# Latent attention of the first token tile split by key tile, with a running maximum, in a two-layer encoder kernel

## The reference

```
h = layer_norm(alpha * h + mixer(h))        # NA in layer 0, MLA in layer 1
hid = gelu(einsum('td,ted->te', h, u[experts]))
h = layer_norm(alpha * h + einsum('te,ted->td', gate * hid, v[experts]))

# MLA, all 16 heads, queries in blocks of 128
q = rms_norm(h @ w_q) @ w_q_up ; k, v = rms_norm(h @ w_kv) @ w_kv_up   (rope on 32 components of q and k)
p = softmax(q k^T * 96**-0.5) ; mix = (p v) @ w_out
```

## Time and profile before

| | us |
|---|---|
| median of 3 runs | 1616.34 (1616.20 to 1616.72) |
| profiled execution, its own time | 1621.26 |
| span of the profiled execution | 1619.5 |
| TensorE busy | 1373.9 (85%) |
| VectorE busy | 1056.7 (65%) |
| ScalarE busy | 476.5 (29%) |
| GpSimd busy | 490.3 (30%) |
| share of the chain that ended last: TensorE / DMA / VectorE | 36% / 34% / 22% |
| bytes read from HBM | 598.96 MB, 371 GB/s over the span |

### The profile page before, as it was taken

The page is one execution under the profiler, slowest core; times in us unless marked ns, Lnnn a source line. Parts: engine busy times, 40 slices in busy tenths (PEclk is TensorE's granted clock), DMA queues, the critical chain, the costliest instruction groups (busy, mean ns, idle before and its releaser), DMA issues.

```text
span 1619.5 us, 16307 instructions
## 1 busy us (share of the span) xinstructions
PE 1373.9 (85%) x5114; PEld 739.9 (46%) x5114; DVE 1056.7 (65%) x2834; ACT 476.5 (29%) x1237; POOL 490.3 (30%) x522
## 2 busy tenths in 40 slices
PE   8999888887878998897789868998877988887876
PEld 7887544433444454443254644444334433433322
DVE  1127777778867766777532477777776876776664
ACT  1122342334323332222123323333332222222222
POOL 0003233333433333333300123333333333333331
PEclk9999999999999999999998989999899999999999
DMA  9528999999999999999961299999999999999996
GB/s 344 189 97 329 387 419 421 418 421 405 398 423 414 420 421 418 417 408 415 419 246 40 94 399 421 407 402 420 420 396 420 420 405 421 421 422 422 412 418 258
DMA packets 92695, 601.09 MB, mean 371 GB/s; under 512 B 10433, under 2 KB 12737, under 8 KB 26433
## 3 DMA queue, kind: packets, MB, share of 16 engines
q0 software_dynamic: 73728, 536.90, 80.7%
q1 hardware_dynamic: 18880, 63.15, 10.1%
HBM read 598.96 MB, written 1.05 MB: 371 GB/s over the span
## 4 chain that ended last, share of the span: by engine, by line
PE 36%; DMA 34%; DVE 22%; issue 4%; ACT 2%; DVEq 2%; POOL 0%; another core or an unknown queue 0%; SPq 0%; POOLq 0%
DMA uv<-in_peer_uv_dram,expert 34%; PE y L554 17%; DVE uv L1417 11%; PE spare L452 3%; PE y L418 3%; PE px L327 2%; PE y L352 2%; ACT diag L1083 1%; DVE key_idx L1324 1%; DVE key_left L1316 1%; DVE key_idx L1318 1%; PE spare L383 1%; PE spare L382 1%; PE spare L369 1%; PE y L409 1%
## 5 line engine op out<-in xcount | busy, mean ns | idle before, releaser
L554 PE MATMUL y<-uv,diag 128*128 128x512 f32 x1928 | 923.4, 619 | 178.4 <-ACT diag L1083 175.1
L1417 DVE CUSTOM_DVE_ANT_0 uv<-px,uv 128x1024 f32<-128x1024 f32 x512 | 618.2, 1220 | 324.6 <-DMA uv<-in_peer_uv_dram,expert 320.3
L965 POOL DMA_INDIRECT uv<-in_peer_uv_dram,expert x512 | 489.1, 955 | 1105.6 <-PE y L554 844.7
L554 PEld LDWEIGHTS y<-uv,diag 128*128 128x128 f32 x1928 | 356.8, 196 | 639.4 <-issue 362.3
L1083 ACT ACTIVATE diag<-ident,wts 128x128 f32<-128x128 f32 x482 | 170.1, 396 | 449.1 <-DVE wts L1423 432.0
L1075 ACT ACTIVATE act_hid<-hid 128x2 f32<-128x2 f32 x260 | 53.4, 205 | 492.1 <-DVE hid L1417 491.8
L1075 ACT ACT_TABLE_LOAD x50 | 64.2, 1283 | 0.9
L398 PE MATMUL spare<-ident,probs 128*128 128x128 f32 x96 | 16.8, 301 | 35.8 <-DVE probs L1263 32.8
L1423 DVE TENSOR_TENSOR wts<-act_hid,gate 128x2 f32<-128x2 f32 x260 | 40.7, 157 | 7.5 <-ACT act_hid L1075 7.5
L1417 DVE DVE_READ_ACCUMULATOR2_ANT hid<- 128x1 f32 x512 | 42.5, 83 | 0.0
L1049 ACT ACT_TABLE_LOAD x30 | 38.5, 1283 | 0.5
(11 more groups left out here) (227 smaller groups left out, 1273.3 us busy)
## 6 DMA issues: line engine op xcount, KB each, us to landing
uv<-in_peer_uv_dram,expert POOLq DMA_INDIRECT x512
wb_rows<-in_peer_w_q_dram SPq DMA_DIRECT2D x16, 512.0 KB
uv<-in_na_w_dram SPq DMA_DIRECT2D x11, 512.0 KB, 8.9
wb_rows<-in_na_w_out_dram SPq DMA_DIRECT2D x8, 512.0 KB
uv<-in_mla_w_out_dram SPq DMA_DIRECT2D x8, 512.0 KB, 10.8
wb_rows<-in_mla_w_out_dram SPq DMA_DIRECT2D x8, 512.0 KB
bias<-in_na_bias_dram SPq DMA_DIRECT2D x16, 160.0 KB, 7.4
w_vu<-in_na_w_dram SPq DMA_DIRECT2D x4, 512.0 KB, 8.5
```

The costliest lines, as they stand in the source:

```text
L554: last = T.matmul(Y[t][:, c, :], diag[:, n % RING, :], uv[:, n % RING, 1, c * 512:(c + 1) * 512], start=False, stop=(k == TOPK - 1 and g % ...
L965: pool.indirect_dma_start(uv[:, n % RING, :, :].rearrange("p h d -> p (h d)"), None, uv_table, bass.IndirectOffsetOnAxis(ap=expert[:, g, k ...
L1417: V_.tensor_tensor_reduce(out=rows, in0=px[:, :, :], in1=rows, scale=1.0, scalar=0.0, op0=ALU.mult, op1=ALU.add, accum_out=hid[:, k:k + 1] ...
```

## The change

MLA of tile 0 is computed in two parts. The scores against tile 0's own 128 keys need nothing of tile 1, so they are made at steps 200 to 247 of layer 0's PEER, four heads ("a quad") every 12 steps: scores in one bank, the maximum per head (`own_nmax`), exponentials and sums (`own_sum`) not divided, transposes, and the product with tile 0's values, kept undivided in SBUF (`own_out`, in the buffer of `vsum`). Between the layers only tile 1's keys are left: scores, a joint maximum of both parts, exponentials against it, a factor exp(own maximum - joint maximum) that scales the kept part and its sum, the new part added, the division by the joint sum, a transpose of the joined 128 x 256 block (now token-major) and the projection. `up_q` of tile 0 moves from between the layers to steps 176 and 180; other latent work of steps 153 to 210 moves by a few steps; `latents_q(1)` is cut in three, two of them between the projections. The SyncE and GpSimd programs are unchanged.

```diff
+QUADS = HEADS // 4
+FIRST = 200
+        S_BANK = [6, 7, 4, 5]
+        T_BANK = [2, 3, 2, 3]
 # TensorE
+            def quad_scores(keys, d, i, b):
+                if i == 0:
+                    bank_free(b)
+                else:
+                    pe.wait_ge(s_even, QUADS * keys + d + 1)
+                where = slice(keys * P, (keys + 1) * P)
+                for e in range(2):
+                    j = 2 * d + e
+                    dst = B[b][:, (2 * e + i) * P:(2 * e + i + 1) * P]
+                    T.matmul(dst, Qm[i * HD:(i + 1) * HD, j, :], Kt[i * HD:(i + 1) * HD, j, where], start=True, stop=False)
+                    last = T.matmul(dst, qpe[i * ROPE:(i + 1) * ROPE, j, :], kpe[i * ROPE:(i + 1) * ROPE, where],
+                                    start=False, stop=True)
...
+            def quad_transposes(keys, d, b, scores_in):
+                pe.wait_ge(s_free[scores_in], job["QS", keys, d])
+                bank_free(b)
+                for h in range(4):
+                    last = T.transpose(B[b][:, h * P:(h + 1) * P], p[:, h, :], ident[:, :])
+            def quad_values(keys, d, b, transposed_in):
+                pe.wait_ge(s_free[transposed_in], job["QT", keys, d])
+                bank_free(b)
+                for h in range(4):
+                    at = (4 * d + h) * HD
+                    last = T.matmul(B[b][:, h * HD:(h + 1) * HD], p[:, h, :], V[:, keys, at:at + HD], start=True, stop=True)
+            def mixed_transposes(d, b):
+                pe.wait_ge(s_mixed, d + 1)
+                for e in range(2):
+                    last = T.transpose(B[b][:, e * P:(e + 1) * P], mixed[d % 2][:, e * P:(e + 1) * P], ident[:, :])
 # side(), layer 0
+                    if at in (176, 180):
+                        up_q(0, (at - 176) // 4, 7)
+                    if at in (187, 190, 193, 196):
+                        up_qpe(0, (at - 187) // 3, 7)
+                    d, r = divmod(at - FIRST, EVERY)
+                    if 0 <= d < QUADS:
+                        if r in (0, 1):
+                            quad_scores(0, d, r, 7)
+                        if r == 6:
+                            quad_transposes(0, d, 7, 7)
+                        if r == 9:
+                            quad_values(0, d, 7, 7)
 # between the layers
-            up_q(0, 0, 4)
             norm_transposes(ffn1, 0, 6)
             norm_transposes(ffn1, 1, 7)
             hT_ready(ffn1, (6, 7))
             latents_kv(1, 2, range(DK))
-            up_q(0, 1, 5)
...
-            gap_scores(0)
+            for i in range(2):
+                for d in range(2):
+                    quad_scores(1, d, i, S_BANK[d])
             up_v(1, 0, 2)
             up_v(1, 1, 3)
             pe.wait_ge(s_free[5], job["upK", 1, 1])
-            gap_scores(1)
-            for j in range(PAIRS):
-                n = pair_no(1, 0, j)
-                transposes(n)
-                if j + 2 < PAIRS:
-                    gap_scores(j + 2)
-                if j:
-                    out_product(n - 1, line_item("O", n - 1))
...
-                weighted_values(n)
-            out_product(n, line_item("O", n))
-            latents_q(1, 4, range(DK))
+            for i in range(2):
+                for d in range(2, 4):
+                    quad_scores(1, d, i, S_BANK[d])
+            quad_transposes(1, 0, T_BANK[0], S_BANK[0])
+            quad_transposes(1, 1, T_BANK[1], S_BANK[1])
+            quad_values(1, 0, S_BANK[0], T_BANK[0])
+            quad_values(1, 1, S_BANK[1], T_BANK[1])
+            mixed_transposes(0, T_BANK[0])
+            quad_product(0)
+            mixed_transposes(1, T_BANK[1])
+            quad_transposes(1, 2, T_BANK[2], S_BANK[2])
+            quad_product(1)
+            quad_transposes(1, 3, T_BANK[3], S_BANK[3])
+            quad_values(1, 2, S_BANK[2], T_BANK[2])
+            quad_values(1, 3, S_BANK[3], T_BANK[3])
+            mixed_transposes(2, T_BANK[2])
+            latents_q(1, 4, range(0, 2))
+            quad_product(2)
+            mixed_transposes(3, T_BANK[3])
+            latents_q(1, 4, range(2, 4))
+            quad_product(3)
+            latents_q(1, 4, range(4, DK))
 # ScalarE: four exps a quad; between the layers
+            def new_exps(d):
+                act.wait_ge(s_joint, d + 1)
+                quad_exps(d, S_BANK[d], joint_nmax, new_sum)
+                four = slice(4 * d, 4 * d + 4)
+                A.activation(own_scale[:, four], own_shift[:, four], ACT.Exp).then_inc(s_new, 1)
...
-            store_up_q(0, 0, 4)
-            store_up_q(0, 1, 5)
-            exps_mla(pair_no(1, 0, 0), gap_banks(0))
+            new_exps(0)
+            new_exps(1)
             store_up_v(1, 0, 2)
+            store_quad_probsT(1, 0, T_BANK[0])
+            store_quad_probsT(1, 1, T_BANK[1])
+            new_exps(2)
+            store_mixedT(0)
+            new_exps(3)
+            fetch_table(ACT.Sqrt)
+            store_mixedT(1)
+            for d in (2, 3):
+                store_quad_probsT(1, d, T_BANK[d])
+            for d in (2, 3):
+                store_mixedT(d)
 # VectorE
+            def joint_max(d):
+                V_.tensor_reduce(new_nmax[:, four], quad(B[S_BANK[d]]), X, ALU.max, negate=True)
+                V_.tensor_tensor(joint_nmax[:, four], new_nmax[:, four], own_nmax[:, four], ALU.min)
+                V_.tensor_tensor(own_shift[:, four], joint_nmax[:, four], own_nmax[:, four], ALU.subtract).then_inc(s_joint, 1)
+            def join(d):
+                dve.wait_ge(s_full[b], job["QV", 1, d])
+                V_.tensor_tensor(mixed[d % 2], B[b][:, 0:4 * HD], mixed[d % 2], ALU.add).then_inc(s_free[b], 1)
+                V_.tensor_tensor(heads, heads, joint_rsum[:, four].unsqueeze(2).broadcast_to([P, 4, HD]), ALU.mult)\
+                  .then_inc(s_mixed, 1)
...
+            joint_max(0)
+            joint_max(1)
             dve.wait_ge(s_full[3], job["upV", 1, 1])
+            scale_own(0)
+            scale_own(1)
+            joint_max(2)
+            joint_max(3)
+            join(0)
+            join(1)
+            scale_own(2)
+            scale_own(3)
+            join(2)
+            join(3)
```

More of the change, by code:

```diff
@@ L389, in scores_mla @@
                     last.then_inc(s_sc0, 1)
+            def quad_scores(keys, d, i, b):
[10 more added lines that the diff above has]
+                                    start=False, stop=True)
+                if i == 0:
+                    last.then_inc(s_even, 1)
+                else:
+                    last.then_inc(s_full[b], 1)
+                    filled(b, ("QS", keys, d))
@@ L1011, in exps_na, with exps_mla @@
                 last.then_inc(s_exp, 1)
[L1013 to L1016, removed]
-                    last = A.activation(probs[n % 2][:, i, :], B[b][:, at:at + TOK], ACT.Exp,
-                                        bias=nmax[:, n % 2, i:i + 1], accum_out=row_sum[:, n % 2, i:i + 1])
-                    if banks[0] != banks[1] or i == 1:
-                        last.then_inc(s_free[b], 1)
+            def exps_mla(n):
+                act.wait_ge(s_max, softmax_no(n) + 1)
+                for i in range(2):
+                    last = A.activation(probs[n % 2][:, i, :], B[6][:, i * TOK:(i + 1) * TOK], ACT.Exp,
+                                        bias=nmax[:, n % 2, i:i + 1], accum_out=row_sum[:, n % 2, i:i + 1])
+                last.then_inc(s_free[6], 1)
@@ new lines, in quad_exps, with own_exps @@
+            def quad_exps(d, b, nmax_of, sum_of):
+                p = quad(probs[d % 2][:, :, :].rearrange("p i n -> p (i n)"))
+                for h in range(4):
+                    col = slice(4 * d + h, 4 * d + h + 1)
+                    last = A.activation(p[:, h, :], B[b][:, h * P:(h + 1) * P], ACT.Exp,
+                                        bias=nmax_of[:, col], accum_out=sum_of[:, col])
+                last.then_inc(s_free[b], 1)
+            def own_exps(d):
+                act.wait_ge(s_own, d + 1)
+                quad_exps(d, 7, own_nmax, own_sum)
@@ new lines, in new_exps, with store_quad_probsT @@
+            def new_exps(d):
[3 more added lines that the diff above has]
+                A.activation(own_scale[:, four], own_shift[:, four], ACT.Exp).then_inc(s_new, 1)
+            def store_quad_probsT(keys, d, b):
+                act.wait_ge(s_full[b], job["QT", keys, d])
+                if keys and d >= 2:
+                    act.wait_ge(s_full[S_BANK[d - 2]], job["QV", 1, d - 2])
+                A.activation(probsT[d % 2][:, :, :, :].rearrange("p i k q -> p (i k q)"), B[b], ACT.Copy)\
+                 .then_inc(s_free[b], 1)
@@ L1444, in side @@
                         else:
-                            softmax_mla(n, (6, 6))
+                            softmax_mla(n)
                     if r == 8:
-                        normalise(n, (6, 6) if layer else None)
+                        normalise(n, slice(0, TOK) if layer else slice(*SEEN[1]))
                 if at == 103:
@@ L1531, in _ @@
```

(4 more changed lines are left out.)

188 lines of the change are left out of this document (115 added, 73 removed).

## The result

The changed kernel takes 1627.46 us (median of 6 runs, 1624.18 to 1631.31) beside 1616.53 for the kernel before on the same chips (6 runs, 1614.94 to 1620.03): a ratio of 1.0066, with a 95% interval of 1.0047 to 1.0084. It is slower by about 11 us, where 8 us of gain were forecast. The profiled execution has a span of 1626.4 us against 1619.5.

A forecast was written before the change was run, and what follows sets the result against it. Gathers were taken to bound the PEER stages and TensorE the stretch between the layers. A gain of 8.3 us there and 0.3 lost under the gathers gave -8.0, from 1616.34 to 1608.3 us, range 1602.5 to 1613.

The forecast's parts named there:

- Under the gathers: Layer 0's PEER steps: added quads and moved latent work hide under the gathers; 0.3 us lost, bounds 0 and 3.
- The third rival: Under the gathers: the quads starve the gathers, 16.6 us lost for 8.3 gained, 1624.7 us; chance 0.05.
- rows 8 and 9: Profile rows under the gathers: DMA share stays 1.01 with TensorE nearly full, and through a TensorE wait of 3.33 us.
- The clock: Attention between the layers: half clock in each score block loses about 6 us, leaving 8.3 gained; bounds 6 and 14.2.
- 41.3 us were worked out: Attention between the layers rebuilt at full clock, first score at 847.5 to end at 888.8, 14.2 us less than before.
- The 0.9 for a quad's values: Attention between the layers: eight value instructions a quad at 0.11 us each, bounds 0.5 and 1.0.
- The 1.3 us: Between the layers: TensorE idles this long, once, for the first join before the first projection.
- the row at 857.4: Trace row of the kernel before: the clock falls between the layers with TensorE busy 2.00 of 2.00 us.
- rival 1: Between the layers: longer score blocks don't lower the clock, or only briefly; gain 11 to 14, 1602.1 to 1605; chance 0.2.
- `up_q`: Between the layers: taking these query products out changes nothing, as they lay in waits for the norm; zero, bounds 0 and 0.3.
- Sum: Whole kernel: -8.3 between the layers plus 0.3 under the gathers gives -8.0 us.

The follow-up runs named there:

- e1: Kernel before with only the change's moved steps for the latent work, nothing else of the change; 1628.79 us, ratio 1.0049.
- e3: Changed kernel with the latent work spaced so TensorE asks for bank 7 after the step at which it is emptied; 1616.73 us, ratio 0.9984.
- e9: Changed kernel with VectorE rotating tile 0's queries two steps earlier, after steps 190, 193, 196 and 199; 1624.25 us, ratio 1.0029.
- e10: Changed kernel with tile 0's key copies one pair of steps earlier on ScalarE and latents_q one step later; 1622.88 us, ratio 1.0020.
- e8: e3 with the quads under the gathers left out, their maximum and sum set to constants; 1619.19 us, ratio 0.9995.
- e13: e5 with the full computation, scores between the layers over all 128 rows from zero-padded queries and rotary keys copied by GpSimd; 1601.22 us, ratio 0.9893.
- e4: Changed kernel with 16 query products repeated, result unused, at each of the two places where up_q stood; 1629.7 us, ratio 1.0054.
- e5: e3 with 16 query products repeated, result unused, at each of the two places where up_q stood; 1616.23 us, ratio 0.9972.
- e11: e5 with full-row score products between the layers, rotary part left out and heads of a pair mixed; 1600.1 us, ratio 0.9883.
- e14: e13 without the repeated query products in the two waits before the scores; 1604.65 us, ratio 0.9908.
- e15: Kernel before, its attention undivided, with zero-padded full-row score products alone; 1605.56 us, ratio 0.9925.
- e6: e5 with one full 128-row product of 512 columns, result unused, after each score call between the layers; 1615.42 us, ratio 0.9974.
- e7: e5 with the same work between the layers interleaved, no scores in blocks of more than 4 us; 1615.42 us, ratio 0.9973.
- e12: e6 with two full products after each score call instead of one; 1621.19 us, ratio 1.0011.

## Why the prediction was wrong

**Moved work, step "Under the gathers".** This is the step that failed. It took the moved copies and latents at nothing because "the moved copies and latents keep their number". Their number wasn't the question. What counted is how many steps lie between the instruction that asks for a bank and the one on another engine that empties it. Before, TensorE asked for the second `up_k` at step 170, and the first was copied after steps 168 and 169. The change asks at 156 for what is copied after 157, at 159 for what is copied after 161, at 172 for what is copied after 173, and at 190 for what is rotated at 192 behind the expert choice. One step ahead is not always paid: the ask at 156 waited 0.21 us, the one at 172 2.14, and the kernel before asks at 194 for what it rotates at 195 and waited 0.02. The two asks that are two steps ahead waited 3.02 and 4.46. The runs showed 10.4 us where 0.3 was taken, with bounds of 0 and 3 (e1, e3, e9, e10). The third rival had the sign and about the size (1624.7) but the wrong place: the quads cost nothing once the waits are gone, as the step said (e8), and rows 8 and 9 were fair evidence for them. They were no evidence for a wait that needs two further steps of dots.

**The clock, step "The clock".** The mechanism was right: the clock fell once in each score block, as said. The size was off. Half-clock time was 20.5 us, where 12 to 16 was taken and 17 was the bound, and the attention took 49.7 us, not 47.2: a gain of 5.9 us where 8.3 was forecast. (The 13.4 us read from before's rows are 13.7.) At full clock the sum was good: 41.3 us were worked out; e13's 34.88 plus 32 products x (0.41 - 0.22) is 41.0. The 0.9 for a quad's values measured 0.85. The 1.3 us that TensorE was to idle before the first projection were less: 0.57, and 0.85 in the whole attention, in the changed kernel, where the slow values cover the join; in e13's attention all idle time together is 1.3.

The prediction set the rule of the Trainium skill ("TensorE: Matmul & The Clock Gate", Part 1), by which an idle TensorE lowers its clock, against the row at 857.4. The row decided rightly: with TensorE busy 49.15 of 50 us, the mean clock was 0.80. By the rule alone it would have been rival 1, 1602 to 1605.

**`up_q`, taken at zero.** The order of the norm's instructions was read rightly, but the products also filled two waits. Without them the clock fell before the first score: 3.4 us at half clock and 1.5 us lost in the changed kernel, 6.8 and 3.0 in e3, none in e4 and e5, which fill the waits again. The 3.0 are also why e3, with the gathers mended, is hardly faster than before.

**Sum.** +10.4 +1.5 -5.9 +1.6 -0.6 = +7.0 for the profiled executions, where -8.0 was forecast. The 1.6 is the half clock under the PEER queries; it is there in some of the traces and not in others (e3 has 19.0 us there, e5 20.6), and no run shows why.

**Open.** What lets the clock fall is narrowed down, not settled. Full-row score products never had a half clock in their blocks (e11, e13, e14, e15), each in one trace; row-restricted ones had it with and without full products between them (e6, e7), and only two full products per call kept it away (e12). In e6 the first block fell and the second, the same sequence, did not. Row-restricted products aren't the only company in which it falls: in the changed kernel it fell under `up_k`, behind short waits, and in e14 some five us behind full-row scores, where e13 runs the same sequence at full clock. So full rows made the half clock rarer here; they are not shown to rule it out. Whether the rows or the switches between row groups decide wasn't tried separately.

## What to carry to other kernels

When work is moved within hand-written step numbers, list for each shared buffer the step at which it is asked for and the step at which another engine empties it, with all that this engine does first; an ask two steps ahead of the copy stopped the gathers for 7 to 9 us here, and one step ahead cost from nothing to 2 us. Check the cost of a stage's products at its own row count before halving their columns, and prefer zero-padded products over all 128 rows where products over 64 and 32 rows alternate. Before work is moved out of a wait of TensorE, ask what the clock does without it: here its absence cost 1.5 to 3 us, though putting work back only moved the half clock to a later stage as long as the scores were row-restricted.

## What was not expected of the hardware

A 32-bit product over 128 columns costs 0.41 us when products over 64 and over 32 rows alternate, and 0.22 us over all 128 rows with the same columns; over 256 columns it is 0.62 and 0.43. The 0.19 us of difference doesn't depend on the columns. Nor does it belong to the restricted rows: it comes with each change of the rows used, and a full product pays it too. In layer 0 of the kernel before, one 128-row product over 128 columns stands alone between two 64-row ones and takes 0.42 us (from 17.20 to the first line below), and in e6 and e12 the full product of 512 columns, 0.86 in a series, takes 1.05 alone and 1.91 in twos:

```profile
17.62 0.54 PE L369 MATMUL spare<-Kt,QQ 64*128 64x160 f32 x2
```

```profile
848.74 1.05 PE y L849 x2
```

```profile
847.43 1.91 PE y L849 x4
```

The Trainium skill ("TensorEngine Tiling (Array Packing)", Tiling Modes, Key Properties) says that a change of tiling mode drains the engine; the runs agree, and 0.19 us per change is what it costs here. Padding pays twice: 32 x 0.19 = 6.1 us and the clock.

Adding 6.9 us of full-array products between the scores (e6 to e12) lengthened the attention by 2.2 us only, since half clock went from 13.7 us to 3.4; the total rose by more, some 6 us by the ratios.
